# A hybrid linear-attention layer on one core: GpSimd instead of VectorE makes the low parts of 56 weight pieces

## The chip, the cores and the metric

The kernel runs on one core of one Trainium2 chip. The metric is the time of one execution on the device in microseconds (us). A core has TensorE (PE in the profile, with its weight loads as PEld), VectorE (DVE), ScalarE (ACT), GpSimd (POOL), SyncE (SP), which here only issues transfers, and 16 DMA engines.

## The reference, cut to what matters

```
h    = rmsnorm(x, norm_w)                   # x is 512 tokens x 2048
proj = h @ w_in                             # 2048 x 7184, split into q, k, v, g of two head groups
o_a  = gated linear attention of 4 heads    # q, k, v, decay from a low-rank projection
o_b  = the same recurrence for 8 heads      # decay from a sigmoid, values from hi
each head is rms-normalised and multiplied by silu(its gate)
out  = rmsnorm(x + concat(o_a, o_b) @ w_out, final_norm_w)
```

All of it is float32.

## The kernel before, in words

**Products in three parts.** TensorE multiplies in a reduced float32 type (fp32r). So each operand is split into a high part (the value rounded to fp32r) and a low part (value minus high part), and each product is made as high x high + high x low + low x high. The activations h_hi and h_lo stay in SBUF. The weights stream: a **piece** is 256 rows x 512 columns of a weight matrix, as a tile of 128 x 1024. For each piece SyncE issues a transfer into `raw` (2 slots), ScalarE writes `w_hi` (L885, 4 slots) and VectorE writes `w_lo = raw - w_hi` (L1296, 4 slots).

**Groups.** Eight pieces make a group, one 2048 x 512 block of weights; TensorE runs 4 chunks of 6 matmuls for each piece (L577). Four counters hold the flow together. `hi_ok` and `lo_ok` count high and low parts made, `piece_done` counts pieces multiplied. ScalarE makes a high part 3 pieces (`LEAD`) ahead of TensorE, once the piece 4 before it is done and the transfer has landed. TensorE waits for `lo_ok` at the start of a piece. SyncE reuses a slot of `raw` once the low part two pieces before has been made.

**Hosted heads.** In groups 4 to 10 (`G_C` to `G_E + 2`, pieces 60 to 115) the work of the 12 attention heads is laid between the pieces. Each engine has a hand-written table that says after which piece, or on TensorE after which chunk, each task of a head stands. On VectorE a group is a loop over the pieces: first `split(G, p)`, the low part of the piece three ahead, then the tasks of step p. TensorE has, for each head, two sets of score products (L630, the second set called level 4 and 5 here), state updates (L643), outputs into `po` (L658, L661), and a mean square (L668). The outputs of a head wait until VectorE has copied the last scores into `att` (L1419), and the level 4 and 5 products wait until VectorE has scaled their operands (L1386, L1387). The six heads of the pairs (groups 8 to 10) have two heads in each group, four pieces each; groups 6 and 7 host two heads each also.

**GpSimd.** It makes masks in the first 12 us. Later it forms sums of weight blocks in DRAM by transfers (L549 copies, L557 accumulating copies), 32 of them for each of three column blocks. Each transfer waits for one more `piece_done` (`pace`), so that they are spread; the 64 of the last two column blocks begin with piece 60.

Of the kernel before, what the change touches and what calls it, by code (L numbers as in the profile page):

```python
# [23 lines left out]
ALU = mybir.AluOpType  # L24
# [17 lines left out]
NP = KT // PK  # L42
RAW, SPL = 2, 4
LEAD = 3
# [43 lines left out]
def first_piece(G):  # L88

    return G * NP if isinstance(G, int) and G < G_C else G * NP + ND  # L90


F_N = first_piece(G_F)
HT = T // 2

OPERANDS = [("S1", 0), ("A11", 0), ("S3", 0), ("S2", 0), ("A11", 1), ("S3", 1), ("A12", 0), ("A22", 0), ("S4", 0),
# [46 lines left out]
def hymba_kernel(nc, x, norm_w, w_in, gla_w_up, gla_b_up, gla_norm_w, lb_logits, hgrn_norm_w, w_out,  # L143
                 final_norm_w, out):
    with ExitStack() as ctx:
# [343 lines left out]
        def _(pool):  # L489
            n = [0]  # L490
# [47 lines left out]
            def pace():  # L538

                pool.wait_ge(piece_done, paced[0])  # L540
                paced[0] += 1

            for pair in (2, 0, 1):
                if pair == 0:
                    paced[0] = D_N + ND
                for j, (name, source) in enumerate(COPIED):
                    for q in range(QP):
                        pace()
                        pool.dma_start(w_sum[pair, j, q], weight_piece(pair, source, q)).then_inc(  # L549
                            w_copied[pair * len(XS) + j], 16)  # L550
                for j, (name, source) in enumerate(ADDED):
                    pool.wait_ge(w_copied[pair * len(XS) + j], 16 * QP)
                    if source in XS:
                        pool.wait_ge(w_added[pair * len(XS) + XS.index(source)], 16 * QP)
                    for q in range(QP):
                        pace()
                        pool.dma_start(w_sum[pair, j, q], weight_piece(pair, source, q), accum_op=ALU.add,  # L557
                                       max_dma_last_dim=4 * PK * GW).then_inc(
                            w_added[pair * len(XS) + j], 16)


        @block.tensor
# [723 lines left out]
        def _(dve):  # L1286
# [13 lines left out]
            def group(G, tasks, take, first=0, last=NP):  # L1300
                for p in range(NP):
                    if first <= p < last:
                        split(G, p)
                    for f in tasks.get(p, ()):
                        f()
                for c in range(4):
                    wait_bank(dve, G, c)
                    take(c)
                for p in range(last, NP):
                    split(G, p)  # L1310
                for f in tasks.get("end", ()):
                    f()
# [335 lines left out]
            def gla_head(h):  # L1648

                return head(gla_at(h), 2 * h, 2 * h + 1, T_GA + h)  # L1650
# [25 lines left out]
            def gla_steps(h, nxt=()):  # L1676
                g = gla_head(h)
                ar, sl, cp = g["arg"], g["scale"], g["scores"]
                todo = {0: [g["args"], g["ends"]] * (h > 0) + [g["early"]], 1: [g["quads"], ar(4), sl(3), ar(5)],
                        2: [cp(0), cp(1), cp(2), sl(4), sl(5), g["states"](0)],  # L1680
                        3: [cp(3)], 5: [g["states"](1), g["cut"]], 7: [g["norm"]]}
                if nxt:
                    todo[6] = [f for x in nxt for f in (x["args"], x["ends"])]
                    todo[7] = [x["early"] for x in nxt] + todo[7]
                return todo

            def shared_steps(h):

                g, s = gla_head(2 + h), hg_head(0, h)
                nxt = gla_head(3) if h == 0 else hg_head(2, 0)  # L1690
                ar, sl, cp = g["arg"], g["scale"], g["scores"]
                ar2, sl2, cp2 = s["arg"], s["scale"], s["scores"]
                return {0: [g["quads"]] * (h == 0) + [ar(4), sl(3), ar(5)],
                        1: [cp(0), cp(1), cp(2), sl(4), sl(5), g["states"](0)],
                        2: [s["args"], s["ends"], cp(3)], 3: [g["states"](1), s["early"], g["cut"]],
                        4: [s["quads"], ar2(4), cp2(0), sl2(3), ar2(5)],
                        5: [cp2(1), cp2(2), sl2(4), sl2(5), s["states"](0), g["norm"]],
                        6: [nxt["args"], nxt["ends"], cp2(3), nxt["early"], s["cut"]], "end": [nxt["quads"], s["norm"]]}

            group(G_C, gla_steps(0), lambda c: None)  # L1700
            group(G_C + 1, gla_steps(1, [gla_head(2)]), lambda c: None)
            group(G_C + 2, shared_steps(0), lambda c: None)
            group(G_C + 3, shared_steps(1), lambda c: None)

            def hg_pair(m, more=True):

# [11 lines left out]
            def gates(e):  # L1718

                def f(c):  # L1720
                    dve.wait_ge(gate_ok, e * 4 + (c + 1))
                    dve.wait_ge(norm_ok, e * 4 + (c + 1) if isinstance(e, int) else 10)
                    o = feat[:, e * 4 + c, :]
                    dve.tensor_tensor(o, o, main[c][:, :], ALU.mult).then_inc(free[c], 1)
                return f

            with dve.Fori(0, 2) as i:
                group(i + G_E, hg_pair(i * 2 + 2), gates(i))
            group(G_E + 2, hg_pair(6, False), gates(2))

            def low(name, b):
                def f():
# [176 lines left out]
```

## Time and profile before

| | before |
|---|---|
| median of 3 runs | 865.1 us (865.01 to 865.16) |
| the profiled execution, own time | 865.03 us |
| its span, first to last instruction | 863.3 us |
| PE busy | 852.0 us, 99% |
| DVE busy | 591.0 us, 68% |
| ACT busy | 423.2 us, 49% |
| POOL busy | 85.2 us, 10% |
| mean granted TensorE clock | 0.997 |

Busy is the time in which an engine has an instruction under way. A matmul of 512 columns is shown with 0.39 us but the next one starts 0.23 us later, so a busy TensorE can still have late starts; these are read from where an instruction starts and what it waited for.

### The profile page before, as it was taken

What the parts mean: (1) busy time and instruction counts of PE and PEld (TensorE: products, weight loads), DVE (VectorE), ACT (ScalarE), POOL (GpSimd) and SP (SyncE); (2) the same over time, 40 slices, a digit from 0 to 9 for tenths busy, and PEclk for the clock granted to TensorE, in tenths of its full rate; (3) what the DMA queues carried; (4) which work ended last, traced back from release to release, by engine and by line L of the source; (5) the groups of instructions that cost most, each with busy time, mean ns of one, the idle gap of its engine ahead of it and who ended that gap; (6) DMA issues with size and microseconds to landing.
All of it is one profiled execution on the core that took longest, in us unless ns stands there. A gap on an engine that the chain in (4) does not pass through costs nothing.

```text
span 863.3 us, 13759 instructions
## 1 busy us (share of the span) xinstructions
PE 852.0 (99%) x5365; PEld 698.8 (81%) x5365; DVE 591.0 (68%) x949; ACT 423.2 (49%) x594; POOL 85.2 (10%) x128
## 2 busy tenths in 40 slices
PE   8999999999999999999999999999999999999996
PEld 5887888888888788888888878888888888888885
DVE  6733476653587747577887978889885669556766
ACT  7521532324455425264465665855655455435454
POOL 4110111110000001011111110000111100000000
PEclk9999999999999999999999999999999999999998
DMA  8276679989654855568776655555777977965554
GB/s 336 66 263 199 173 198 232 197 196 245 224 191 138 275 173 183 184 169 172 153 177 138 157 169 180 150 174 156 163 168 156 279 168 267 346 199 193 195 171 195
DMA packets 75459, 167.75 MB, mean 194 GB/s; under 512 B 7365, under 2 KB 15593, under 8 KB 74505
## 3 DMA queue, kind: packets, MB, share of 16 engines
q1 hardware_dynamic: 45554, 108.02, 37.9%
q0 software_dynamic: 16896, 50.34, 27.4%
q10 hardware_dynamic: 12952, 8.61, 3.4%
q8 instruction: 38, 0.62, 0.3%
q14 instruction: 19, 0.16, 0.1%
HBM read 158.56 MB, written 58.72 MB: 252 GB/s over the span
## 4 chain that ended last, share of the span: by engine, by line
PE 90%; DVE 5%; ACT 2%; issue 1%; DMA 1%; ACTq 0%; DVEq 0%
PE main L577 57%; PE main L837 8%; PE main L773 5%; PE sc L837 4%; PE sc L630 2%; PE st L837 2%; PE po L837 2%; PE po L658 2%; PE st L643 1%; PE sc L773 1%; PE po L661 1%; DVE w_lo L1296 1%; PE main L689 1%; DMA raw<-in_w_in 1%; PE st L773 1%
## 5 line engine op out<-in xcount | busy, mean ns | idle before, releaser
L577 PE MATMUL main<-h_hi,w_hi 128*128 128x512 f32 x640 | 254.2, 397 | 0.1
L577 PE MATMUL main<-h_hi,w_lo 128*128 128x512 f32 x640 | 249.7, 390 | 0.0
L577 PE MATMUL main<-h_lo,w_hi 128*128 128x512 f32 x640 | 249.3, 390 | 0.0
L1296 DVE TENSOR_TENSOR w_lo<-raw,w_hi 128x1024 fp32r<-128x1024 f32 x100 | 122.1, 1221 | 118.6 <-ACT w_hi L885 118.2
L885 ACT ACTIVATE w_hi<-raw 128x1024 fp32r<-128x1024 f32 x100 | 105.6, 1057 | 188.8 <-PE main L577 132.2
L577 PEld LDWEIGHTS main<-h_hi,w_lo 128*128 128x128 f32 x640 | 120.1, 188 | 25.8
L577 PEld LDWEIGHTS main<-h_hi,w_hi 128*128 128x128 f32 x640 | 120.2, 188 | 25.5 <-issue 0.5
L577 PEld LDWEIGHTS main<-h_lo,w_hi 128*128 128x128 f32 x640 | 120.3, 188 | 23.7
L907 ACT ACTIVATE ex<-ex 128x512 f32<-128x512 f32 (+2 forms) x84 | 52.0, 640 | 21.4 <-DVE ex L1434 14.7
L577 PE MATMUL main<-w_hi,h_hi 128*128 128x512 f32 x128 | 51.4, 402 | 0.0
L577 PE MATMUL main<-w_lo,h_hi 128*128 128x512 f32 x128 | 50.5, 394 | 0.0
L577 PE MATMUL main<-w_hi,h_lo 128*128 128x512 f32 x128 | 50.4, 394 | 0.0
L1774 DVE TENSOR_TENSOR w_lo<-feat,w_hi 128x1024 fp32r<-128x1024 f32 x26 | 31.7, 1224 | 26.9 <-ACT w_hi L1219 26.6
L549 POOL DMA_DIRECT2D w_sum<-in_w_out x32 | 21.0, 657 | 261.1 <-PE main L577 185.8
L1219 ACT ACTIVATE w_hi<-raw 128x1024 fp32r<-128x1024 f32 x27 | 28.6, 1060 | 33.2 <-PE main L837 17.3
L1774 DVE TENSOR_TENSOR w_lo<-raw,w_hi 128x1024 fp32r<-128x1024 f32 x27 | 33.0, 1223 | 15.0 <-ACT w_hi L1219 14.9
L1219 ACT ACTIVATE w_hi<-feat 128x1024 fp32r<-128x1024 f32 x26 | 27.4, 1059 | 31.3 <-PE main L837 15.4
L958 ACT ACTIVATE feat<-po 128x512 f32<-128x512 f32 (+1 forms) x16 | 9.6, 599 | 46.8 <-PE po L661 46.8
L557 POOL DMA_DIRECT2D w_sum<-w_sum x24 | 19.7, 821 | 125.3 <-PE main L577 111.0
L837 PE MATMUL main<-w_hi,s_hi 128*128 128x512 f32 x80 | 31.1, 389 | 0.0
L837 PE MATMUL main<-w_lo,s_hi 128*128 128x512 f32 x80 | 31.1, 389 | 0.0
L837 PE MATMUL main<-w_hi,s_lo 128*128 128x512 f32 x80 | 31.1, 389 | 0.0
(314 smaller groups left out, 1496.5 us busy)
## 6 DMA issues: line engine op xcount, KB each, us to landing
raw<-in_w_in SPq DMA_DIRECT2D x102, 512.0 KB, 4.6
w_sum<-in_w_out POOLq DMA_DIRECT2D x48, 512.0 KB, 5.2
w_sum<-in_w_in POOLq DMA_DIRECT2D x24, 512.0 KB, 5.6
w_sum<-w_sum POOLq DMA_DIRECT2D x24, 512.0 KB, 6.2
raw<-w_sum SPq DMA_DIRECT2D x24, 512.0 KB, 4.2
feat<-w_sum SPq DMA_DIRECT2D x24, 512.0 KB, 4.1
raw<-in_w_out SPq DMA_DIRECT2D x14, 512.0 KB, 4.7
feat<-in_w_out SPq DMA_DIRECT2D x10, 512.0 KB, 4.7
```

The costliest lines, as they stand in the source:

```text
L549: pool.dma_start(w_sum[pair, j, q], weight_piece(pair, source, q)).then_inc(w_copied[pair * len(XS) + j], 16)
L557: pool.dma_start(w_sum[pair, j, q], weight_piece(pair, source, q), accum_op=ALU.add, max_dma_last_dim=4 * PK * GW).then_inc(w_added[pair * ...
L577: mm = pe.matmul(main[c][:, :], a, b, start=(k == 0 and j == 0), stop=(k == KT - 1 and j == 2))
L630: mm = pe.matmul(into[l][b * BW:b * BW + m, to:to + w], kl[KL[l]][:, c * P + b * BW:c * P + b * BW + m], (eq4 if l in (1, 2) else queries( ...
L658: mm = pe.matmul(po[:, cs], vs(xx)[:, c, :], att[:, cs], start=True, stop=(c == 0))
L773: mm = pe.matmul(d_banks[bank][a][:, :], left, right, start=(q == 0 and kk == 0 and j == 0 and idx not in D_ADDS), stop=(q == QP - 1 and k ...
L837: mm = pe.matmul(banks[other or bank][a][:, cols], left, right, start=(k == 0 and j == 0 and idx not in ADDS_ON), stop=(k == KT // 2 - 1 a ...
L885: act.activation(w_hi[:, q % SPL, :, :], (first_raw if first else raw)[:, q % RAW, :, :], ACT.Copy).then_inc(hi_ok, 1)
L907: act.activation(dst, src, ACT.Exp, scale=scale).then_inc(exp_ok, 1)
L1219: act.activation(w_hi[:, q, :, :], src, ACT.Copy).then_inc(hi_ok, 1)
L1296: dve.tensor_tensor(w_lo[:, q % SPL, :, :], (first_raw if first else raw)[:, q % RAW, :, :], w_hi[:, q % SPL, :, :], ALU.subtract).then_in ...
L1774: dve.tensor_tensor(w_lo[:, q, :, :], src, w_hi[:, q, :, :], ALU.subtract).then_inc(lo_ok, 1)
```

## The change

In pieces 63 to 118, `LOWS`, the low part is made by GpSimd. These are the pieces whose low parts VectorE made inside groups 4 to 10. VectorE's `group` gets `first = NP` for them and so makes none there. GpSimd makes each one right behind the paced transfer with the same count, after waiting for ScalarE's `hi_ok`. VectorE waits for `lo_ok` of piece 118 before it goes on with piece 119. Same values, same slots; TensorE, ScalarE and SyncE have the same instructions as before.

```diff
+LOWS = range(first_piece(G_C) + LEAD, first_piece(G_E + 3) + LEAD)
...
+            def low_part(n):
+
+                if n not in LOWS:
+                    return
+                if n == LOWS[0]:
+                    pool.wait_ge(lo_ok, n)
+                q = n - first_piece(G_C)
+                pool.wait_ge(hi_ok, n + 1)
+                pool.tensor_tensor(w_lo[:, q % SPL, :, :], raw[:, q % RAW, :, :], w_hi[:, q % SPL, :, :],
+                                   ALU.subtract).then_inc(lo_ok, 1)
...
                         pool.dma_start(w_sum[pair, j, q], weight_piece(pair, source, q)).then_inc(
                             w_copied[pair * len(XS) + j], 16)
+                        low_part(paced[0] - 1 + LEAD)
...
                                        max_dma_last_dim=4 * PK * GW).then_inc(
                             w_added[pair * len(XS) + j], 16)
+                        low_part(paced[0] - 1 + LEAD)
...
-            group(G_C, gla_steps(0), lambda c: None)
-            group(G_C + 1, gla_steps(1, [gla_head(2)]), lambda c: None)
-            group(G_C + 2, shared_steps(0), lambda c: None)
-            group(G_C + 3, shared_steps(1), lambda c: None)
+            group(G_C, gla_steps(0), lambda c: None, NP)
+            group(G_C + 1, gla_steps(1, [gla_head(2)]), lambda c: None, NP)
+            group(G_C + 2, shared_steps(0), lambda c: None, NP)
+            group(G_C + 3, shared_steps(1), lambda c: None, NP)
...
-                group(i + G_E, hg_pair(i * 2 + 2), gates(i))
-            group(G_E + 2, hg_pair(6, False), gates(2))
+                group(i + G_E, hg_pair(i * 2 + 2), gates(i), NP)
+            group(G_E + 2, hg_pair(6, False), gates(2), NP)
+            dve.wait_ge(lo_ok, LOWS[-1] + 1)
```

GpSimd's program from piece 60 on, before: transfers only, each behind a count of pieces.

```order
L549 DMA w_sum<-in_w_out 256x1x512 [waits piece_done] x16
L557 DMA w_sum<-in_w_out 256x1x512 [waits piece_done,w_copied0]
L557 DMA w_sum<-in_w_out 256x1x512 [waits piece_done] x3
L557 DMA w_sum<-in_w_out 256x1x512 [waits piece_done,w_copied1]
L557 DMA w_sum<-in_w_out 256x1x512 [waits piece_done] x3
```

And GpSimd's program from piece 60 on, with the change (line 561 was 549).

```order
L561 DMA w_sum<-in_w_out 256x1x512 [waits piece_done]
L552 TENSOR_TENSOR w_lo<-raw,w_hi 128x1024 [waits hi_ok,lo_ok]
L561 DMA w_sum<-in_w_out 256x1x512 [waits piece_done]
L552 TENSOR_TENSOR w_lo<-raw,w_hi 128x1024 [waits hi_ok]
L561 DMA w_sum<-in_w_out 256x1x512 [waits piece_done]
```

A subtraction of 128 x 1024 now stands between every two of these transfers, 56 in all, so that a transfer is issued only after the subtraction before it.

On VectorE the place is the second head of a pair, from its last level arguments (`ex<-bcum`) over the scan for the next head (`bcum`) to the copies of its first scores. Before:

```order
L1362 TENSOR_TENSOR ex<-bcum 128x4x64 [waits lvl_ok]
L1363 TENSOR_TENSOR ex<-bcum 128x4x64
L1424 REGISTER_ALU
L1426 REGISTER_ALU [waits arg_ok]
L1427 SCALAR_TENSOR_TENSOR bcum<-reset,gdec 128x512 [waits g_ok]
L1294 REGISTER_ALU
L1296 TENSOR_TENSOR w_lo<-raw,w_hi 128x1024 [waits hi_ok]
L1400 COPY_PREDICATED att<-mask,sc 128x512 [waits sc_ps]
```

The same place with the change (line numbers are 14 higher).

```order
L1376 TENSOR_TENSOR ex<-bcum 128x4x64 [waits lvl_ok]
L1377 TENSOR_TENSOR ex<-bcum 128x4x64
L1438 REGISTER_ALU
L1440 REGISTER_ALU [waits arg_ok]
L1441 SCALAR_TENSOR_TENSOR bcum<-reset,gdec 128x512 [waits g_ok]
L1414 COPY_PREDICATED att<-mask,sc 128x512 [waits sc_ps]
```

The subtraction and its wait for `hi_ok` are gone from between the scan and the copies; the rest keeps its order.

## Rows read from the trace of the kernel before

**Rows 1.** Page, part 1, share of the span by engine

```profile
PE 852.0 (99%) x5365; PEld 698.8 (81%) x5365; DVE 591.0 (68%) x949; ACT 423.2 (49%) x594; POOL 85.2 (10%) x128
```

**Rows 2.** Windows of two pair groups: us, then busy us, PEclk, DMA share, GB/s

```profile
496.00:549.00 53.00, 52.79 (x491) 43.02 (x490) 44.00 (x93) 33.24 (x54) 5.31 (x8) 1.00 0.54 170
549.00:603.00 54.00, 54.00 (x499) 44.40 (x497) 46.64 (x97) 33.61 (x55) 5.21 (x8) 1.00 0.54 165
```

**Rows 3.** Waits of TensorE: total us, times, longest

```profile
PE po L658 <- DVE att L1419: 0.5, 2, 0.3
PE st L601 <- DVE kd L1449: 0.5, 1, 0.5
```

**Rows 4.** Page, part 5: VectorE's low parts, busy, mean ns, idle before

```profile
L1296 DVE TENSOR_TENSOR w_lo<-raw,w_hi 128x1024 fp32r<-128x1024 f32 x100 | 122.1, 1221 | 118.6 <-ACT w_hi L885 118.2
```

**Rows 5.** Timeline of VectorE, second head of a pair (start, us)

```profile
526.71 1.22 DVE L1296 TENSOR_TENSOR w_lo<-raw,w_hi 128x1024 fp32r<-128x1024 f32 x1
527.85 0.69 DVE L1348 TENSOR_TENSOR kl<-feat,kl 128x512 f32<-128x512 f32 x1
...
532.95 1.20 DVE L1296 TENSOR_TENSOR w_lo<-raw,w_hi 128x1024 fp32r<-128x1024 f32 x1
534.07 0.73 DVE L1400 COPY_PREDICATED att<-mask,sc 128x512 f32<-128x512 uint8 x1
...
537.56 0.42 DVE L1386 TENSOR_TENSOR kl<-feat,ex 128x256 f32<-128x256 f32 x1
...
538.57 0.41 DVE L1387 TENSOR_TENSOR ql<-feat,ex 128x256 f32<-128x256 f32 x1
```

**Rows 6.** Timeline of ScalarE, the same head: high parts and one exponential

```profile
525.63 1.05 ACT L885 ACTIVATE w_hi<-raw 128x1024 fp32r<-128x1024 f32 x1
...
526.58 0.62 ACT L907 ACTIVATE kl<-kl 128x512 f32<-128x512 f32 x1
...
530.13 1.05 ACT L885 ACTIVATE w_hi<-raw 128x1024 fp32r<-128x1024 f32 x1
...
537.04 1.06 ACT L885 ACTIVATE w_hi<-raw 128x1024 fp32r<-128x1024 f32 x1 [4.70 <-PE main L577]
```

**Rows 7.** Timeline of TensorE, the same head: level 4 and 5 products

```profile
539.65 0.94 PE L630 MATMUL sc<-ql,kl 128*16 128x16 f32 x64
```

**Rows 8.** Timeline of GpSimd, first 9 us: sizes

```profile
3.69 0.52 POOL L511 TENSOR_SCALAR_AFFINE_SELECT gdec<-gdec 128x128 f32<-128x128 f32 x1
4.27 0.29 POOL L513 CAST mask<-gdec 128x128 uint8<-128x128 f32 x1
...
6.17 0.40 POOL L521 CAST mask<-gdec 128x256 uint8<-128x256 f32 x1
```

**Rows 9.** Timeline of GpSimd and VectorE, 6 to 11 us

```profile
6.81 0.19 POOL L527 TENSOR_SCALAR_AFFINE_SELECT gdec<-gdec 128x8 f32<-128x8 f32 x1
...
8.01 0.69 DVE L1522 COPY feat<-main 128x512 f32<-128x512 f32 x1 [1.01 <-PE main L689]
8.27 0.19 POOL L529 TENSOR_SCALAR_AFFINE_SELECT gdec<-gdec 128x8 f32<-128x8 f32 x1
...
8.81 1.41 DVE L1509 SCALAR_TENSOR_TENSOR feat<-feat,rs 128x512 f32<-128x512 f32 x2
9.03 0.10 POOL L526 MEMSET gdec<- 128x8 f32 x1
9.20 0.41 POOL L527 TENSOR_SCALAR_AFFINE_SELECT gdec<-gdec 128x8 f32<-128x8 f32 x1
9.68 0.59 POOL L529 TENSOR_SCALAR_AFFINE_SELECT gdec<-gdec 128x8 f32<-128x8 f32 x1
10.14 1.22 DVE L1296 TENSOR_TENSOR w_lo<-raw,w_hi 128x1024 fp32r<-128x1024 f32 x1
10.34 1.07 POOL L532 CAST mask_q<-gdec 128x8 uint8<-128x8 f32 x1
```

**Rows 10.** Low part 63 on VectorE, and GpSimd's paced transfers

```profile
289.34 1.23 DVE L1296 TENSOR_TENSOR w_lo<-raw,w_hi 128x1024 fp32r<-128x1024 f32 x1 [4.24 <-ACT w_hi L885]
...
297.41 0.65 POOL L549 DMA_DIRECT2D w_sum<-in_w_out  x1 [5.87 <-PE main L577]
...
530.08 0.65 POOL L549 DMA_DIRECT2D w_sum<-in_w_out  x1 [5.51 <-PE main L577]
```

## The prediction

> **What bounds the kernel now.** I read the page first: TensorE has an instruction under way for 99% of the span, VectorE for 68%, GpSimd for 10% [rows 1]. The windows of the groups that host heads say the same more sharply: in the stretch from 549 to 603 us TensorE is busy 54.00 of 54.00 us at full granted clock, while VectorE, at 46.64 us, is the next fullest [rows 2]. So TensorE bounds the kernel, and a change on another engine shows only in how often TensorE starts late. The waits of TensorE name two such places on VectorE, 0.5 us in all for the copies into `att` and 0.5 us for one `kd` [rows 3]. That is 1.0 us in 863.3: taking work off VectorE has very little to win here, however full VectorE is. The other question is how near VectorE comes to making TensorE late. In the second head of a pair the scaling that the level 4 and 5 products need ends at 538.57 + 0.41 = 538.98 us [rows 5], and TensorE takes the products up at 539.65 [rows 7]. The margin is 0.67 us.
>
> The executions differ by 0.15 us, but I take 0.2% (1.7 us) as the least difference that can be told. The sum is made against the profiled execution, 865.03 us with a span of 863.3; it lies 0.1 us below the median, so that the same sum holds for both.
>
> **What the change removes.** 56 subtractions leave VectorE. One is 1.221 us long [rows 4] and holds up the next instruction by 1.14 (526.71 to 527.85) or 1.12 us (532.95 to 534.07) [rows 5]: 56 x 1.14 = 64 us of VectorE time. VectorE also stops waiting for ScalarE's high parts (118.2 us over all 100) [rows 4]. Off the path nearly all of it; at most the 1.0 us above comes back.
>
> **What it adds to GpSimd.** The trace has no subtraction of two tensors on GpSimd, so I bound it. A cast of 128 x 128 takes 0.29 us and one of 128 x 256 takes 0.40 [rows 8]: 0.86 ns an element and 0.18 us fixed. With 1024 elements that gives 1.06 us for one source operand, the lower bound. Two operands read one after the other give 0.18 + 1024 x 1.72 ns = 1.94 us. The costliest row an element is a select of 128 x 128 at 0.52 us [rows 8], 2.66 ns an element, which gives 2.9 us, the upper bound. I take 2.0 us, since a subtraction of two tensors is nearest to two casts.
>
> The Trainium skill ("GPSIMD Engine Reference", section "Performance versus the Vector engine") gives 4497 ns on GpSimd and 2293 ns on VectorE for a two-input add of 2048 elements. Its ratio of 1.96 on the 1.221 us of [rows 4] would make the subtraction 2.4 us, and by it the sum below would come to about 888 us.
>
> **Whether TensorE runs out of pieces.** GpSimd goes in order: transfer, wait for the high part, subtraction. The transfer occupies it for 0.65 us [rows 10]. The closest piece is the first, 63: before, its low part ran from 289.34 to 290.57, and TensorE reached the piece at 297.41, when the paced transfer of that count went out [rows 10]. With 2.0 in place of 1.2 us some 6 us of margin are left; even 2.9 us leave 5. A piece of a pair group takes 53/8 = 6.6 us, and 2.0 + 0.65 fit into it. I cost this at nothing; the cover is the lead of three pieces. The transfers of the weight sums go out up to 2 us later, behind the subtraction; nothing needs them before the output products, which follow the hosted groups.
>
> **What the two engines do to each other.** This decides the case. GpSimd's small selects take 0.19 us alone, and also when VectorE copies from PSUM (8.27 us). At 9.20 and 9.68 us, beside a VectorE instruction with two SBUF operands, they take 0.41 and 0.59; a cast issued at 10.34 lasts 1.07 us, until 11.41, just after VectorE's subtraction of 10.14 + 1.22 = 11.36. A memset, which reads nothing, takes its 0.10 at 9.03 beside the same kind [rows 9]. So something on the way to SBUF is held by a VectorE instruction with two SBUF sources until it ends. The rows show GpSimd held and never VectorE, because GpSimd's operands there have 8 elements. I take the holding to be mutual: while GpSimd reads 1024 elements twice, a VectorE instruction with two SBUF sources waits to the end.
>
> The Trainium skill ("SBUF — State Buffer", section "Who interferes with whom") states this as a rule: VectorE with two SBUF inputs contends with a GpSimd instruction that reads SBUF, the one that comes first keeps the shared ports for its whole length and the other blocks. The trace agrees for GpSimd blocked (0.19 against 0.59 us); VectorE blocked is not shown. By the rule this change loses.
>
> Worked out for the second head of a pair. GpSimd's subtraction follows each high part, which end at 526.68, 531.18 and 538.10 [rows 6].
> - The first holds VectorE from 526.7 to 528.7. The scaling L1348, which needs an exponential ended at 527.20 [rows 6] and began at 527.85 behind the removed subtraction [rows 5], now begins at 528.75: 0.9 late.
> - The second falls into a dense run of two-source instructions: 2.0 us, less the 1.12 of the removed subtraction at 532.95. Now 0.9 + 2.0 - 1.1 = 1.8 late.
> - The copies into `att` read their data from PSUM and are not held; they ran from 534.07 to 537.56 [rows 5] and now end at 539.3. The third holds until 540.2: 0.9 more.
>
> Level 4 and 5 operands are ready at 538.98 + 2.7 = 541.7, and TensorE, due at 539.65, starts 2.0 us late. In the first head of a pair the third subtraction lies wholly under the copies, which leaves 2 x 2.0 - 2.3 = 1.7. Mean 1.8 us, six heads: 10.8 us. The delay does not carry over, since ScalarE's next tasks start from TensorE's and VectorE has an idle stretch in each head. The four heads of groups 6 and 7 have a little more margin, an estimate of 1.0 us each: 4. The first two heads have an engine half idle: nothing. The `kd` wait and half of the `att` waits go: -0.8. Sum: 10.8 + 4 - 0.8 = **+14 us, 879 us**.
>
> With 1.06 us for a subtraction the savings outweigh the holding and nothing is late: 864 us. With 2.9 each head loses 2 to 3 us more: about 900 us.
>
> **Rivals.**
> 1. *VectorE is not held* (GpSimd alone gives way, as in all of [rows 9]). Its subtractions stretch to perhaps 4 us, inside the 5 to 6 us of cover. The two waits of [rows 3] go: 864.0 us, no difference to tell. Chance 0.22.
> 2. *The same, and faster.* With low parts out of VectorE's order, small late starts that the wait view gives no name to close as well. Only 863.3 - 852.0 = 11.3 us are without TensorE work [rows 1], most of it ahead of the hosted groups and behind them; if twice the named 1.0 us comes back it is 863.0 us. It decides from 1.7 us gained. Chance 0.13.
> 3. *TensorE waits for low parts*: a subtraction plus its holding over 6 us, against a piece of 6.6. Against it stands the lead of three pieces. 56 pieces at 0.5 us late would be 893 us. Chance 0.05.
> 4. *Forecast*: VectorE held, heads late. 879 us, its own range 868 to 890. Chance 0.60.
>
> **How the numbers follow.** The likeliest case is the forecast, 879. The range has to reach the rivals on the lower side, 863, and 889 above; what is left out is the upper bound of the subtraction, most of rival 3 and gains above 2 us. Faster by over 0.2% is rival 2, 0.13. Within it is rival 1, 0.22. Slower is the rest, 0.65.
>
> **What would show it.** In the profile after: a GpSimd group `w_lo<-raw,w_hi` x56 with a mean of about 2 us, longer where it meets VectorE. VectorE's two-source instructions such as L1348 lengthened from 0.69 to up to 2.7 us, its PSUM copies unchanged. New waits of TensorE on VectorE in front of L630 and L658 of 1 to 2 us a head. TensorE on `w_lo` should not wait at all. If two-source instructions on VectorE keep their lengths under a GpSimd subtraction, the forecast is wrong and it is rival 1 or 2. If GpSimd's subtraction is near 1 us, the sign of the sum falls away too.

## The result and the profile after

The changed kernel takes 891.37 us (median of 6 runs, 885.59 to 892.69) against 865.06 (864.56 to 865.32) for the kernel before, run beside it: a ratio of 1.0292, with a 95% interval of 1.0277 to 1.0308. It is slower by 26 us, and no longer regular: the six executions of the kernel before agree within 0.8 us; those of the changed kernel lie up to 7 apart. The profiled execution is the quickest of the six (885.59 us, span 883.9), so I account for it first and for the spread in a step of its own.

The page after, part 1 and the two groups that touch `w_lo` (to be set against [rows 1] and [rows 4]):

```profile
PE 855.0 (97%) x5365; PEld 700.0 (79%) x5365; DVE 600.0 (68%) x893; ACT 423.2 (48%) x594; POOL 223.6 (25%) x184
L552 POOL TENSOR_TENSOR w_lo<-raw,w_hi 128x1024 fp32r<-128x1024 f32 x56 | 140.3, 2505 | 110.4 <-ACT w_hi L899 110.2
```

GpSimd's subtraction takes 2.5 us on the average, where I took 2.0. VectorE has 56 instructions fewer and is still busy for 68% of the span: what it was rid of it got back as longer instructions. TensorE's waits, by line and releaser (total us, times, longest), where [rows 3] had 1.0 us in all (the wait for `val` is at the start of the kernel and was 2.5 us before):

```profile
PE sc L644 <- DVE ql L1401: 14.0, 9, 2.1
PE main L703 <- DMA val<-in_norm_w: 2.7, 1, 2.7
PE sc L644 <- DVE ex L1365: 2.2, 1, 2.2
PE po L672 <- DVE att L1433: 1.6, 4, 0.4
PE main L591 <- ACT feat L1078: 0.6, 1, 0.6
```

The level 4 and 5 products (L644, L630 before) wait for the scaled operands nine times. `POOL w_lo L552` is not in the list: no product waits for a low part of GpSimd. The next two fences are the same second head of a pair as in [rows 5] and [rows 6], first VectorE, then GpSimd. Columns: start, duration, engine, line and operation, and idle time ahead in brackets.

```profile
538.33 2.48 DVE L1362 TENSOR_TENSOR kl<-feat,kl 128x512 f32<-128x512 f32 x1 [0.59 <-ACT kl L921]
...
543.20 2.62 DVE L1376 TENSOR_TENSOR ex<-bcum 128x256 f32<-128x256 f32 x1
545.75 0.41 DVE L1377 TENSOR_TENSOR ex<-bcum 128x256 f32<-128x256 f32 x1
...
549.80 1.20 DVE L1427 COPY_PREDICATED att<-mask_q,po 128x192 f32<-128x192 uint8 x3 [0.23 <-DVE att L1427]
550.91 1.06 DVE L1400 TENSOR_TENSOR kl<-feat,ex 128x256 f32<-128x256 f32 x1
```

```profile
537.86 2.41 POOL L552 TENSOR_TENSOR w_lo<-raw,w_hi 128x1024 fp32r<-128x1024 f32 x1 [1.46 <-ACT w_hi L899]
541.21 0.66 POOL L561 DMA_DIRECT2D w_sum<-in_w_out  x1 [0.94 <-PE main L591]
543.14 2.40 POOL L552 TENSOR_TENSOR w_lo<-raw,w_hi 128x1024 fp32r<-128x1024 f32 x1 [1.28 <-ACT w_hi L899]
...
549.32 2.38 POOL L552 TENSOR_TENSOR w_lo<-raw,w_hi 128x1024 fp32r<-128x1024 f32 x1 [0.22 <-ACT w_hi L899]
```

Read one against the other. The scaling L1362 (L1348 before, 0.69 us) begins at 538.33 under the subtraction that runs from 537.86 to 540.27, and ends at 540.81: 0.54 us after it. L1376, 0.41 us by itself (as L1377 beside it), begins at 543.20 and ends at 545.82, 0.28 us after the second subtraction (545.54). The third begins at 549.32; the copies with data from PSUM keep their 1.20 us under it, and only L1400 behind them is held, to 551.97 (0.27 us after 551.70). TensorE's rows of this place, first the 32 products that need earlier operands only, then the 32 that need the held scaling:

```profile
550.79 0.39 PE L644 MATMUL sc<-ql,kl 128*16 128x16 f32 x32
553.11 0.65 PE L644 MATMUL sc<-ql,kl 128*32 128x32 f32 x32 [1.94 <-DVE ql L1401]
```

It waits 1.94 us ahead of the second row. The profile of after has one more thing that the one of before lacks. Windows ahead of, in and behind a stretch in the first such head (length, busy us and instructions by engine, granted clock, DMA share, GB/s):

```profile
520.00:524.40 4.40, 2.45 (x72) 1.75 (x70) 3.66 (x12) 0.00 (x0) 2.34 (x1) 1.00 0.53 141
524.47:527.88 3.41, 3.41 (x9) 2.63 (x10) 3.34 (x9) 2.79 (x7) 0.30 (x1) 0.50 0.34 130
528.00:531.40 3.40, 3.40 (x24) 3.05 (x23) 3.13 (x8) 0.74 (x2) 0.24 (x1) 1.00 0.57 153
```

After a wait of 1.95 us that ended at 523.76, the granted clock is 0.50 (1.2 GHz) for 3.41 us and then full again. The counts of the last two rows, 9 and 24 products, cannot be set against each other, since 14 of the 24 are short ones (L672, L675). What the stretch costs is read from the products of 512 columns: in it they start 0.43 us apart, at full clock 0.23. So 3.41 us at half clock do what takes 1.8 us at full clock, and 1.6 us are lost (worked out from these distances).

### The profile page after: what moved, and what is told of

The parts are those of the page before. It is cut to its first block, busy times and chain, and to the rows that moved or that the text cites. A ratio compares the mean times of both kernels' runs of the same rounds, so it can differ in the third digit from the quotient of the medians.

```text
span 883.9 us, 13746 instructions
## 1 busy us (share of the span) xinstructions
PE 855.0 (97%) x5365; PEld 700.0 (79%) x5365; DVE 600.0 (68%) x893; ACT 423.2 (48%) x594; POOL 223.6 (25%) x184
## 4 chain that ended last, share of the span: by engine, by line
PE 71%; DVE 14%; issue 7%; ACT 6%; DVEq 1%; ACTq 0%; DMA 0%
PE main L591 40%; PE main L851 8%; PE main L787 5%; PE sc L851 4%; DVE att L1427 2%; PE st L851 2%; PE po L851 2%; PE po L672 2%; DVE ql L1401 2%; PE st L787 1%; PE po L787 1%; PE sc L787 1%; PE po L675 1%; DVE kl L1388 1%; DVE ex L1377 1%
## 5 line engine op out<-in xcount | busy, mean ns | idle before, releaser
L552 POOL TENSOR_TENSOR w_lo<-raw,w_hi 128x1024 fp32r<-128x1024 f32 x56 | 140.3, 2505 | 110.4 <-ACT w_hi L899 110.2
L1310 DVE TENSOR_TENSOR w_lo<-raw,w_hi 128x1024 fp32r<-128x1024 f32 x44 | 53.8, 1224 | 86.4 <-ACT w_hi L899 86.3
L1789 DVE TENSOR_TENSOR w_lo<-raw,w_hi 128x1024 fp32r<-128x1024 f32 x27 | 32.9, 1222 | 14.8 <-ACT w_hi L1233 14.7
L561 POOL DMA_DIRECT2D w_sum<-in_w_in x16 | 10.6, 663 | 95.1 <-PE main L591 95.1
L644 PEld LDWEIGHTS sc<-ql,kl 128*32 128x32 f32 (+1 forms) x1152 | 13.4, 105 | 23.1 <-issue 13.8
```

Source lines behind the costliest of these rows:

```text
L552: pool.tensor_tensor(w_lo[:, q % SPL, :, :], raw[:, q % RAW, :, :], w_hi[:, q % SPL, :, :], ALU.subtract).then_inc(lo_ok, 1)
L1310: dve.tensor_tensor(w_lo[:, q % SPL, :, :], (first_raw if first else raw)[:, q % RAW, :, :], w_hi[:, q % SPL, :, :], ALU.subtract).then_in ...
L1789: dve.tensor_tensor(w_lo[:, q, :, :], src, w_hi[:, q, :, :], ALU.subtract).then_inc(lo_ok, 1)
```

## The experiments

My theory (A): while GpSimd reads SBUF, VectorE's instructions with two SBUF sources stand until it ends, and where the subtraction falls in a head decides what it costs. Its rivals: (B) the loss is from the order, from GpSimd's queue or from late pieces; (D) every moved subtraction costs the same, wherever it stands. Later came (C): waits that long also lower the clock. The kernel before, run beside each of them, took 864.2 to 866.0 us.

**No low parts at all.** 

```diff
-                pool.tensor_tensor(w_lo[:, q % SPL, :, :], raw[:, q % RAW, :, :], w_hi[:, q % SPL, :, :],
-                                   ALU.subtract).then_inc(lo_ok, 1)
+                pool.memset(w_lo[:, q % SPL, 0, 0:8].bitcast(F32), 0.0).then_inc(lo_ok, 1)
```

> In the changed kernel, GpSimd's 56 subtractions are replaced by memsets of 128 x 8 in w_lo with the same waits and the same place in its program, so that these low parts are left out of the products (VectorE does not make them either). Theory A (a GpSimd instruction that reads SBUF holds VectorE's two-source instructions to its end): with nothing to hold, TensorE's new waits in front of the level 4 and 5 products (14.0 us in the changed kernel) are gone, 863.5 to 865 us, L1362 back at 0.69 us. Rival B (the new order of GpSimd's program or of VectorE's does the harm, such as transfers that go out late or low parts counted on another engine): order and counters are those of the changed kernel, so it stays above 870 us. What is left under 865.06 is what taking the work off VectorE is worth: at most 1.0 us by the prediction.

Measured: 862.74 us, ratio 0.9978 (0.9968 to 0.9987). All waits, semaphores and queue positions of the change are kept, and it is quicker than before, so that of B the order and the queue fall. Its memsets are short, so late pieces are left to the next run. (One of the eleven executions took 3021.57 us; no row says why, and the median leaves it out.) It also gives what the work taken off VectorE is worth: 2.1 us, twice the 1.0 us of [rows 3] and more than I had expected.

**GpSimd busy, but only writing.** 

```diff
-                pool.tensor_tensor(w_lo[:, q % SPL, :, :], raw[:, q % RAW, :, :], w_hi[:, q % SPL, :, :],
-                                   ALU.subtract).then_inc(lo_ok, 1)
+                for _ in range(2):
+                    step(pool.memset(w_lo[:, q % SPL, :, :].bitcast(F32), 0.0))
+                pool.memset(w_lo[:, q % SPL, :, :].bitcast(F32), 0.0).then_inc(lo_ok, 1)
```

> As e1, but GpSimd is kept busy in the place of each subtraction, for longer than the subtraction's 2.4 us, and reads nothing: three memsets of the whole 128 x 1024 tile, one after the other, some 3 us by the 0.20 and 0.31 us that 128 and 256 columns took. The low parts of these pieces are zeros. Theory A: VectorE is not held by writes, 863.5 to 866 us. Rival B (GpSimd's length itself, late transfers, late slots of raw): as slow as the changed kernel or slower, 890 us and more. Rival C (any access of GpSimd to SBUF disturbs VectorE): slower, 875 to 890 us, with longer L1362.

Measured: 863.02 us, ratio 0.9979 (0.9969 to 0.9988). Two rows of VectorE and the GpSimd rows beside them:

```profile
524.95 0.69 DVE L1363 TENSOR_TENSOR kl<-feat,kl 128x512 f32<-128x512 f32 x1 [0.59 <-ACT kl L922]
525.80 1.09 DVE L1366 TENSOR_TENSOR ex<-feat,ex 128x384 f32<-128x384 f32 x3 [0.16 <-ACT ex L922]
```

```profile
524.45 1.97 POOL L553 MEMSET w_lo<- 128x1024 f32 x2 [0.91 <-ACT w_hi L900]
526.48 0.95 POOL L554 MEMSET w_lo<- 128x1024 f32 x1
```

GpSimd is at work from 524.45 to 527.43, 3.0 us against the 2.4 of the change, and the scaling keeps its 0.69 us. So the last part of B, pieces that come late by GpSimd's length, falls too. GpSimd's time is not what costs; its reading is.

**One source instead of two.** Two casts of `raw` into `w_lo` for each subtraction (the first in place, the second with the `then_inc`):

```diff
-                pool.tensor_tensor(w_lo[:, q % SPL, :, :], raw[:, q % RAW, :, :], w_hi[:, q % SPL, :, :],
-                                   ALU.subtract).then_inc(lo_ok, 1)
+                step(pool.tensor_copy(w_lo[:, q % SPL, :, :], raw[:, q % RAW, :, :]))
+                pool.tensor_copy(w_lo[:, q % SPL, :, :], raw[:, q % RAW, :, :]).then_inc(lo_ok, 1)
```

> As e1, but in the place of each subtraction GpSimd copies raw into w_lo twice, one after the other, so that it reads one tensor at a time, some 2.1 us in all by 0.29 and 0.40 us for casts of 128 and 256 columns. What is computed is not the layer (the low parts are whole weights). Theory A: each copy holds VectorE's two-source instructions to its own end, with a gap between the two in which one VectorE instruction can slip in: level 4 and 5 products 1 to 2 us late a head, 875 to 888 us. If reading one source does not hold VectorE, 864 to 866 us. Rival B: 885 us or more, by GpSimd's length alone.

Measured: 870.32 us, ratio 1.0062 (1.0047 to 1.0078): under the 875 to 888 that I had expected. TensorE waits for L1401 five times, 6.0 us in all. VectorE and GpSimd at one of them:

```profile
539.71 1.25 DVE L1401 TENSOR_TENSOR ql<-feat,ex 128x256 f32<-128x256 f32 x1
540.89 0.41 DVE L1400 TENSOR_TENSOR kl<-feat,ex 128x256 f32<-128x256 f32 x1
```

```profile
538.47 1.04 POOL L552 CAST w_lo<-raw 128x1024 fp32r<-128x1024 f32 x1 [0.21 <-ACT w_hi L899]
539.58 1.11 POOL L553 CAST w_lo<-raw 128x1024 fp32r<-128x1024 f32 x1
```

A cast (a mean of 1.14 for the first and 1.17 us for the second) holds VectorE as well: L1401 takes 1.25 us in place of 0.41, beside a cast that runs until 540.69. But two casts are two holds of some 1.1 us with a gap between them in which VectorE gets on, and one of the two often meets nothing. I had counted the two as one long hold.

**The same subtraction in four pieces.** 

```diff
-                pool.tensor_tensor(w_lo[:, q % SPL, :, :], raw[:, q % RAW, :, :], w_hi[:, q % SPL, :, :],
-                                   ALU.subtract).then_inc(lo_ok, 1)
+                for k in range(4):
+                    at = slice((k % 2) * GW // 2, (k % 2 + 1) * GW // 2)
+                    mm = pool.tensor_tensor(w_lo[:, q % SPL, k // 2, at], raw[:, q % RAW, k // 2, at],
+                                            w_hi[:, q % SPL, k // 2, at], ALU.subtract)
+                mm.then_inc(lo_ok, 1)
```

> The changed kernel, each of GpSimd's subtractions cut into four of 128 x 256, nothing left out. Theory A (held to the end of one GpSimd instruction): the longest L1362 falls from 2.48 us to 0.69 plus one quarter, about 1.4 us, and VectorE's instructions alternate with the quarters; since a dense run of VectorE waits for a quarter before each of its instructions, what it loses in a run of seven stays near 2.4 us, so 880 to 892 us. If instead GpSimd and VectorE share by element, the lengths of L1362 stay as they are, near 2.4 us.

Measured: 894.51 us (892.43 to 896.57), ratio 1.0341 (1.0321 to 1.036); slightly above what was expected. VectorE and GpSimd in the same head:

```profile
540.49 0.82 DVE L1365 TENSOR_TENSOR kl<-feat,kl 128x512 f32<-128x512 f32 x1 [0.59 <-ACT kl L924]
541.34 2.61 DVE L1368 TENSOR_TENSOR ex<-feat,ex 128x384 f32<-128x384 f32 x3
```

```profile
540.01 3.78 POOL L554 TENSOR_TENSOR w_lo<-raw,w_hi 128x256 fp32r<-128x256 f32 x4 [1.07 <-ACT w_hi L902]
```

The scaling now takes 0.82 us, not 2.48: a hold ends with the GpSimd instruction, and the hold goes by instruction, not by share of the time. But the next quarter takes its turn: three instructions of VectorE behind it take 2.61 us (1.08 in the kernel as changed), the four quarters 3.78 us. Finer pieces move the loss and add to it: TensorE waits 19.1 us for L1404 (L1401 in the change, 14.0 us), and this profile has four stretches at half clock where that of the change has one.

**Which of the four steps of a head.** GpSimd makes the low parts of some of every four steps, VectorE the others, in order on `lo_ok`.

```diff
+ON_DVE = (0, 1)
...
-                if n not in LOWS:
+                if n not in LOWS or (n - LOWS[0]) % 4 in ON_DVE:
                     return
-                if n == LOWS[0]:
+                if n == LOWS[0] or (n - LOWS[0] - 1) % 4 in ON_DVE:
                     pool.wait_ge(lo_ok, n)
...
+                    elif first == NP and p % 4 in ON_DVE:
+                        split(G, p, (p - 1) % 4 not in ON_DVE)
```

With `ON_DVE = (0, 1, 2)`, so that 14 of the 56 are moved:

> The kernel before, with GpSimd making the low part in one of every four steps, the fourth (p = 3 and 7 of a group), 14 pieces; VectorE makes the other 42 in their old places. In the pair groups VectorE is idle or copies from PSUM for some 3 us after that step's high part. Theory A says that only where a hold falls matters: here it falls into the idle stretch, so 864 to 866 us. If each GpSimd subtraction had the same price wherever it stands, 14 of 56 would cost a quarter of 26 us: 871.5 us.

With `(0, 1)`, as shown (28 moved):

> As e7, with GpSimd making the third and the fourth of every four steps, 28 pieces. With VectorE keeping the first two it reaches the scaling of levels 4 and 5 when it did before, and the third step's hold (2.4 us from ScalarE's high part on) now meets it: the first head of a pair some 1.0 us late, the second 1.6 us, so six heads 8 us and 2 for the shared groups: 875 us by theory A. By equal prices 878 us.

With `(2, 3)` (28 moved, the others):

> The mirror of e6: GpSimd makes the first and second of every four steps, 28 pieces, VectorE the third and fourth. Both holds that make the scaling late are there, and both saved subtractions too. Theory A: TensorE nearly as late in front of levels 4 and 5 as in the changed kernel, and VectorE's third subtraction is back in front of the copy for the outputs: 884 to 891 us. By equal prices it equals e6 at 878 us.

| GpSimd makes | moved | us | ratio (95%) |
|---|---|---|---|
| the fourth | 14 | 864.73 | 1.0001 (0.9992 to 1.0011) |
| third and fourth | 28 | 871.51 | 1.0090 (1.0070 to 1.0109) |
| first and second | 28 | 882.12 | 1.0201 (1.0185 to 1.0217) |
| all | 56 | 891.37 | 1.0292 (1.0277 to 1.0308) |

The fourth alone came out as expected; third and fourth 3.5 us below the 875 that I had expected, first and second 1.9 us below its 884 to 891. Under D the first row would be 871.5 and the two middle ones equal. They are not: the fourth subtraction, which falls where VectorE is not the last to be ready, costs nothing; the first two, ahead of the scaling and in the dense run, most. TensorE's waits of the first-and-second kernel show what it keeps of the change:

```profile
PE sc L645 <- DVE ql L1406: 6.9, 6, 1.6
PE po L673 <- DVE att L1438: 3.5, 8, 0.5
...
PE sc L645 <- DVE ex L1370: 2.2, 1, 2.2
```

**Is it the length of the wait that lowers the clock?** Six products of no use (into a bank that is rewritten) stand ahead of the wait for the level 4 operands, so that TensorE is not idle in it:

```diff
                     def f():
+                        if l == 4:
+                            pe.wait_ge(sc_ok, H * NEAR + 3)
+                            for _ in range(6):
+                                pe.matmul(sc[0][:, :], h_hi[:, 0, 0:P], h_hi[:, 0, :], start=True, stop=True)
                         pe.wait_ge(lvl_ok, H * NL + (l + 1))
...
```

> The changed kernel, with six matmuls of 128 x 512 (1.4 us) on TensorE ahead of each head's wait for its level 4 operands; they multiply activations into a PSUM bank that the level 4 products then overwrite, so nothing is left out. The changed kernel's profiled execution waited 1.1 to 2.1 us there and has one stretch of 3.41 us at half clock 0.7 us behind a wait of 2.1 us; five others of its executions took 888.7 to 892.7 us with mean clocks of 0.990 to 0.995. Theory C (TensorE's idle waits let its clock fall, and that is the part of the loss beyond the waits): with waits of under 0.8 us the clock stays at 0.996 or 0.997 in every execution and the times gather at 884 to 887 us, 5 us under the changed kernel's median. If the clock has another cause, the spread stays and the median is 890 us or more, since the filler takes some time in the two heads that wait less.

Measured: 891.05 us (889.01 to 892.22), ratio 1.0304 (1.0289 to 1.0318). The waits before L1406 (L1401) shrink to 1.1 us, and the mean granted clock is 0.996 to 0.998 in every run, where the change has 0.990 to 0.996. The profile still has one stretch at half clock, and it stands 0.6 us behind the start of the product that ended the one long wait left, which the filler does not cover (TensorE, then the window):

```profile
395.42 0.38 PE L649 MATMUL sc<-ex,kl 128*32 128x48 f32 x16 [2.20 <-DVE ex L1370]
```

```profile
396.03:399.44 3.41, 3.41 (x12) 2.93 (x13) 2.91 (x9) 1.26 (x2) 0.00 (x0) 0.50 0.86 238
```

So far C holds. The time does not follow: 12 x 6 products of 0.227 us are 16.3 us, of which only 12.9 lie in waits that would have been there. The 3.4 us left over eat what the clock gives back. On the time the expectation was missed: 891.05 us is what I had expected if the clock had another cause, and five executions still lie 3.2 us apart at nearly one mean clock. So the clock is not the whole of the spread.

**The same lateness without GpSimd.** In the kernel before, VectorE makes the low parts of the first and second of every four steps twice:

```diff
+                if twice and p % 4 < 2:
+                    dve.tensor_tensor(w_lo[:, q % SPL, :, :], raw[:, q % RAW, :, :], w_hi[:, q % SPL, :, :],
+                                      ALU.subtract).then_inc(made_once, 1)
+                    dve.wait_ge(made_once, G * 4 + (p // 4 * 2 + p % 4 + 1 - 4 * G_C))
...
```

> The kernel before, GpSimd untouched; VectorE makes the low part twice at the first and second of every four steps of the hosting groups (28 more subtractions at 1.14 us each hold up what follows), nothing is left out. So VectorE has 2.28 us at each place where e8 gave it a hold of 2.4 us, and everything else as e8. Theory A (a hold is VectorE time lost at that place and nothing else): TensorE waits for levels 4 and 5 as in e8, 879 to 884 us against e8's 882.1. If GpSimd's reading costs in another way also (ScalarE, transfers, TensorE), this stays well under e8, 872 us or less. Theory C (the clock falls behind TensorE's waits): stretches at half clock of 3.41 us here too if a wait reaches 2.1 us, though GpSimd does nothing new.

Measured: 889.82 us, ratio 1.0290 (1.0275 to 1.0304); missed, 5.8 us above the upper end of what was expected. TensorE waits 10.3 us for L1392 and 7.1 us for the copies into `att`, where the first-and-second kernel had 6.9 and 3.5. I had set 1.2 us of own work equal to 1.2 us of hold. My reading, which no run tests by itself, is that a hold costs only where a two-source instruction meets it, while own work always costs. That GpSimd's reading costs in some further way (872 us or less here) is refuted. The run does bear on C:

```profile
526.27 0.65 PE L631 MATMUL sc<-ql,kl 128*32 128x32 f32 x32 [2.39 <-DVE ql L1392]
```

```profile
523.00:526.40 3.40, 1.01 (x47) 0.56 (x49) 2.78 (x10) 0.00 (x0) 0.00 (x0) 1.00 0.57 181
526.90:530.31 3.41, 3.41 (x10) 2.73 (x9) 3.38 (x7) 2.40 (x7) 0.16 (x1) 0.50 0.20 30
646.40:649.81 3.41, 3.41 (x9) 2.62 (x9) 3.38 (x8) 2.40 (x5) 1.03 (x1) 0.50 0.35 86
```

The clock falls to 0.50 for 3.41 us behind waits of 2.39 and 1.64 us (the second ended at 645.08), with no work of the change on GpSimd. The fall belongs to TensorE's waiting, whoever causes it. Not every such wait has one: in the same kernel a wait of 1.82 us at 586.26 is followed by full clock (1.00 in both windows behind it, to 594), and so are four waits in the profile of after, of 2.20, 1.94, 1.94 and 2.14 us (ended at 392.42, 553.11, 611.00 and 668.70), and in the quarters two of 2.80 and 3.07 us (401.96, 586.78). So the length of a wait alone does not tell whether the clock falls.

**The changed kernel again**, with no edit, for the spread:

> The changed kernel once more, on another chip or another day, for its clock: theory C expects the profile to show one to four stretches of 3.41 us at half clock, each within 1.5 us behind the start of the product that ended a wait of 2 us or more, and the executions to spread from 885 to 893 us with the mean clock going down as the time goes up, 1.7 us for each stretch. If the spread is that of the chip and not of the waits, the kernel before would spread as much on this chip; it has spread 1.9 us over 21 runs so far.

Measured: 890.28 us (884.83 to 892.43), ratio 1.0279 (1.0254 to 1.0304). The kernel before, on the same chip, took 864.4 to 865.6 us, so the spread belongs to the changed kernel, as expected. This time the profiled execution is a long one (891.59 us, span 889.3). Its one long wait that the first profile does not have is in the very first head (VectorE and TensorE, then windows of a later place):

```profile
305.00 3.08 DVE L1401 TENSOR_TENSOR ql<-feat,ex 128x256 f32<-128x256 f32 x1
...
308.81 0.65 PE L644 MATMUL sc<-ql,kl 128*32 128x32 f32 x32 [2.43 <-DVE ql L1401]
```

```profile
392.50:395.90 3.40, 1.20 (x43) 1.10 (x39) 3.40 (x5) 0.52 (x1) 2.02 (x1) 1.00 1.03 247
396.00:399.41 3.41, 3.41 (x11) 2.64 (x10) 2.69 (x8) 0.65 (x2) 0.00 (x0) 0.50 0.65 196
```

A subtraction of GpSimd ran from 305.30 to 307.79, and L1401 ends at 308.08, 0.29 us after it, though it had begun at 305.00, ahead of it. In the first profile the subtraction began at 306.10, when the last scaling had all but run (305.74 to 306.15), and held none of them. And there are two stretches at half clock in place of one, the one shown, 1.3 us behind the end of a wait of 2.20 us, and one from 672.50, where a wait of 2.15 us was about to end (672.65).

**From the experiments a version that is not slower.** In the kernel before, the third low part of each four steps is made behind the copy into `att` at L1419 in groups 6 to 10; GpSimd is left alone:

```diff
-                    if first <= p < last:
+                    if first <= p < last and p not in behind:
                         split(G, p)
-                    for f in tasks.get(p, ()):
+                    for n, f in enumerate(tasks.get(p, ())):
                         f()
+                        if n + 1 == behind.get(p):
+                            split(G, p)
...
-            group(G_C + 2, shared_steps(0), lambda c: None)
+            group(G_C + 2, shared_steps(0), lambda c: None, behind={2: 3, 6: 3})
...
```

> The kernel before with all low parts on VectorE; in groups 6 to 10 the subtraction of the third of every four steps stands behind the copy of the last scores (L1419) in place of ahead of it. TensorE's starts on the outputs, late by 0.2 to 0.6 us in five heads by start-to-start times, are then met: 863.6 to 864.6 us, under the 0.2% that can be told, perhaps 0.1% under the kernel before. It is the part of e1's 2.1 us that order alone gives.

Measured: 863.72 us, ratio 0.9988 (0.9979 to 0.9997). All that is left of TensorE's waits:

```profile
PE main L689 <- DMA val<-in_norm_w: 2.6, 1, 2.6
PE main L837 <- DVE w_lo L1776: 0.4, 1, 0.4
```

The waits of [rows 3] are gone, for 1.1 us. It is the quickest kernel here that computes everything. Its 0.1% is less than the 0.2% that I had set as the least difference that can be told, though the interval leaves out 1; it is about half of what the removal of all 56 subtractions would be worth.

## Why the prediction was right in its way and too low

**Right: sign and mechanism.** The hold is mutual, as I took it to be. It ends with GpSimd's instruction (538.33 + 2.48), spares copies with data from PSUM, and does not exist for writes (863.02 us). TensorE does not run out of pieces, and GpSimd's queue costs nothing (862.74). Rival 1 (VectorE not held) is refuted by the 2.48 us, rival 3 by a wait view in which no product waits for GpSimd's `w_lo`. Rival 2 had the value of the relief nearly right, 2.1 us against its 2.0, and fell with rival 1.

The Trainium skill ("SBUF — State Buffer", section "Who interferes with whom") has this rule; the runs now agree in the direction that the trace of before could not show, 2.48 against 0.69 us, and in that writes do not take part. What the Trainium skill says there of which one has to wait, the one that comes second, the profile's times do not bear out in every case: L1401 at 305.00 in the second profile began 0.30 us ahead of GpSimd's subtraction and was held to that subtraction's end all the same (starts on GpSimd are rough in a profile).

**Term by term**, for the profiled execution (span 883.9 against 863.3, so +20.6; predicted +14). The waits are TensorE's, head by head.

| term | predicted | measured |
|---|---|---|
| six heads of pairs (groups 8 to 10) | 10.8 | 1.95 + 1.94 + 1.56 + 1.94 + 1.35 + 2.14 = 10.9 |
| four heads of groups 6 and 7 | 4 | 7.6 |
| first two heads | 0 | 0 (2.4 in the second profile) |
| waits that go | -0.8 | -1.0 |
| clock | none | 1.6 |
| rest, which no view names | none | 1.5 |

Of the 12.4 us between the 879 forecast and the median of 891.4, 6.6 are missing from the sum for the profiled execution (20.6 against 14), and 5.8 lie between that execution and the median.

The sum that I worked out in full came to within 0.1 us, with a subtraction that was too short, and part of that is luck. Measured from the end of the exponential (527.20 before, 538.30 after), VectorE's scaling is 1.2 us late behind the first subtraction (0.9 by my working) and the copies into `att` 2.3 us late behind the second (1.8), but the third subtraction met only L1400 for 0.65 us, where I gave it 0.9. That makes the operands 2.9 us late, not 2.7. The margin, in turn, was larger than my 0.67 us. Only the last 32 of the 64 products of [rows 7] need this scaling (in TensorE's rows after the change the first 32 start at 550.79, before L1400 has begun); before, these 32 started at 539.94, 0.96 us behind the scaling. The two errors nearly cancel: in the one head worked out TensorE waits 1.94 us against 2.0.

**Wrong, the first step: "The four heads of groups 6 and 7 have a little more margin, an estimate of 1.0 us each: 4."** The level 4 and 5 products there wait 1.14, 0.98 and 1.04 us, as said, in three of four. But each of the four also waits 0.39 to 0.45 us for its outputs (L672), 1.6 in all; once the scaling for the first products is held (L1365, 2.2 us, at 392.42), and once ScalarE's `feat` is late (0.6). So this term measured 7.6 us where I had 4: I had worked out one place in a head and taken the rest of these four heads from an estimate that no row bore.

**Wrong, the second: "it lies 0.1 us below the median, so that the same sum holds for both".** That was so before (0.15 us of spread) and was not after. The kernel before, which hardly waits, takes no notice of a shift of 0.8 us; one in which GpSimd's instruction just hits or just misses does. The median lies 5.8 us above the profiled execution. The second profile's span is 5.4 us longer than the first's: one wait of 2.4 us in the first head, one more clock stretch of 1.6, and small waits for the rest. So the first two heads, which I cost at nothing, gave nearly half of it. With the mean clock falling from 0.996 to 0.992 or less in four of the six runs, which is about two more stretches of 3.41 us (3.2 us), and one such wait, I arrive at 5.6 of the 5.8. For the unprofiled executions that is an estimate from their mean clock, not shown; and the mean clock is a rough measure (one execution of the first-and-second kernel has 0.946 and is no slower than the others).

**Left out altogether: the clock.** In the hosted groups of the kernel before TensorE never waits for more than 0.5 us, so they have no row of it; that trace is at half clock only in its last 4.5 us, behind TensorE's last product. Ahead of the end the stretches stand in six profiles: after, its second profile, the quarters, the first-and-second kernel, the filler and the doubled work on VectorE. With the waits filled the mean clock goes back up, and the profiles whose waits behind the start are all under 1.5 us (before and the other six) have no stretch. That the fall goes with TensorE's waits is shown; why one wait of 1.64 us has it and others of 2.80 and 3.07 don't stays open.

**The two source operands.** I took 2.0 us as the sum of two casts; a cast of 1024 takes 1.04 us at its shortest, near my lower bound of 1.06, and the subtraction 2.40, more than two of them. The Trainium skill ("GPSIMD Engine Reference", section "Performance versus the Vector engine") gave 2.4 us by its ratio, which the trace meets: 36 of the 56 subtractions take 2.38 to 2.44 us, and the mean is 2.5. By it the sum came to "about 888 us", inside my range. That sum happens to be nearer, but for a part of the reason only: the heads that I worked out did not grow with it.

## What to carry to other kernels

Work moved from VectorE to GpSimd is not taken off VectorE if it reads SBUF: ask of each two-source VectorE instruction that may fall under it whether TensorE waits for it, and move only what falls where the answer is no (864.7, 871.5 and 882.1 us for three choices of place). Before moving, look whether the order alone gives what there is to gain (863.72 us here, 0.1%). And where a change makes TensorE wait for about 2 us at a time, expect some of these waits to cost more than their length, and profile more than one execution.

## What the runs showed of the hardware

- On 128 x 1024 f32 GpSimd takes 2.40 us for a subtraction of two SBUF tensors (mean 2.5 beside VectorE), 1.14 to 1.17 for a cast, 0.95 to 0.98 for a memset; on 128 x 256 a subtraction takes 0.72 us at its shortest and 0.89 in the mean. VectorE takes 1.22 for the subtraction of 1024.
- A VectorE instruction with two SBUF sources that begins under a GpSimd instruction that reads SBUF ends 0.2 to 0.6 us after it, and a scan of 1.22 us 1.1 us after it (0.69 becomes 2.48, 0.41 becomes 2.62). An instruction of VectorE that by the profile began up to 0.35 us ahead of GpSimd's was held as well (305.00 in the second profile, 0.41 becomes 3.08). A cast with one source holds it too (0.41 becomes 1.25). A memset does not (0.69 stays 0.69), and a predicated copy whose data come from PSUM is not held, though its mask lies in SBUF (1.20 stays 1.20).
- GpSimd's subtraction is held in turn. In the profile of after its longest, 3.50 us, begins at 344.94 under a row of VectorE's two-source instructions that ends at 346.19 (first fence: VectorE, second: GpSimd). The next instruction of VectorE is held, to 0.28 us after the subtraction's end at 348.44.
- Even a small copy of VectorE with one SBUF source was held, twice in the profile of after: L1466, 0.16 us elsewhere in the trace, took 2.36 beside a subtraction that ended at 411.70, and again at 469.63. I had expected that of two-source instructions alone.

```profile
345.77 0.42 DVE L1389 TENSOR_TENSOR ql<-feat,ex 128x256 f32<-128x256 f32 x1
346.22 2.50 DVE L1376 TENSOR_TENSOR ex<-bcum 128x256 f32<-128x256 f32 x1
...
409.36 2.36 DVE L1466 COPY dec<-ex 128x2 f32<-128x2 f32 x1
```

```profile
344.94 3.50 POOL L552 TENSOR_TENSOR w_lo<-raw,w_hi 128x1024 fp32r<-128x1024 f32 x1 [2.29 <-ACT w_hi L899]
...
408.89 2.81 POOL L552 TENSOR_TENSOR w_lo<-raw,w_hi 128x1024 fp32r<-128x1024 f32 x1 [3.02 <-ACT w_hi L899]
```

- The granted clock went to 0.50 for 3.41 us at a time, eleven times in six profiles (after, its second profile, the quarters, the first-and-second kernel, the filler, the doubled work on VectorE), each beginning between 0.2 us ahead of and 1.5 us behind the end of a wait of TensorE of 1.64 to 2.8 us, whether VectorE was late by GpSimd's doing or by its own. Waits of up to 3.07 us were passed without it. In such a stretch products of 512 columns start 0.43 us apart in place of 0.23.
